# Scan decays of the prompt: running sums as head rows in two parts, one-hot and identity products, exponential straight from the bank

## The chip, the cores and the metric

The kernel runs as one program on 1 core of a Trainium2 chip. The metric is the device time of the program in microseconds (us). TensorE (PE in the profile; PEld for its weight loads), VectorE (DVE), ScalarE (ACT), GpSimd (POOL) and the DMA engines work side by side; each runs its own list of instructions in order and waits for others through semaphores.

## The reference, cut to what matters

One layer of a hybrid decoder, for a prompt of 256 tokens and 8 sample tokens. The change concerns the state-space branch of the prompt. It has 32 heads in 4 groups, a head width of 64, and chunks of 128 tokens:

```python
acum = cumsum(dt * a)                         # per head, within a chunk
seg = acum[t] - acum[s]
decay = exp(where(t >= s, seg, -inf))
wts = cb[t, s] * decay * dt[s]                # cb: product of C and B, per group
y_diag = wts @ x
decay_end = exp(acum[-1] - acum)
states = B^T (decay_end * dt * x);  h = h * exp(acum[-1]) + states
y = y_diag + (C h_prev) * exp(acum) + d * x
```

The kernel treats the 256 prompt tokens as one chunk, which gives the same values: a head then has a 256 x 256 lower triangle of decays, cut into three 128 x 128 blocks. With s on the partitions they are s in the first half against t in the first and in the second half, and s in the second half against t in the second. Beside this the layer has window attention, attention over a memory, gates, an output projection and a mixture of 32 experts (two for each token).

## The kernel before

All activations are kept transposed, with features on the partitions and 264 tokens (256 + 8) in a row. Weights come in chunks of 1 MB (256 columns) into three buffers W, loaded by SyncE in the order of use. The order of all work is written out by hand, engine by engine; `opened`, `full`, `drains`, `wait_filled` and `wait_drained` hand the eight matmul banks over between the engines.

**Split tiles.** The products with the memory weights and with the x/B/C, k, q and mq columns are computed in float32r, in two parts. For each 128 columns ScalarE makes the high part (`highs`, L1264), and GpSimd (`lows`) or, for some, VectorE (`vector_lows`) subtracts it from the weight to make the low part (`low_part`, L229). TensorE then makes 3 x 8 products (L469), and ScalarE copies the result out (`evac`, L1237). The normed inputs are split in the same way by VectorE (L1510, L1511); the first split tile waits for `mem_normed`, which the low part of the memory input gives. The columns of z and of the gates use plain float32 (L457).

**`rstd`** (L1239) is used 23 times: it loads a table set, then takes Ln of a sum of squares in a bank, then Exp. Each call has a table load at L1242.

**The scan stage** lies in the loop over the 40 tiles of z and the gates, TensorE's at L785, with its counterparts at L1344 (ScalarE) and L1758 (VectorE). Step i on TensorE: the tile zg i (eight products, L457); for i < 8 `ssd_bcast(i)`; for 1 <= i < 9 `ssd_y(i - 1)`; for i < 12 the two products `qk(i)` (L628, L630). A unit u is four heads. In it:

- `ssd_bcast` (L596) spreads dt*a of a head over all partitions as a weight and multiplies it with the triangle table: the running sum of the head, as a row, in every partition. Two heads share a bank, in banks 3 and 4.
- VectorE's `segments` (L1635) subtracts the running sum of the partition's own token (AC) and limits the result at 0, eight operations for a unit, into a tile D in S (two buffers).
- ScalarE takes the exponential of all of D (1536 columns) in one instruction (L1350), after copying out the tile zg i, and goes on to `rstd` of the q/k squares, for which it waits for VectorE's `qk_ready` of the step before.
- VectorE's `decays` (L1656), at the start of the next step, multiplies D with CB. CB is the product of C and B, already multiplied with the triangle at L1632.
- `ssd_y` (L609) multiplies D with XD, 64 columns of weights a head, and VectorE's `y_add` adds it to C. Then VectorE rotates q or k (`rotate`, L1669), which needs `rstd`.

At i = 10 to 13 TensorE makes the end states (L640), which wait for XD weighed by VectorE (L1771). At i = 12 and 13 the mq columns are normed: squares on TensorE (L478), four `rstd`, two VectorE products each (L1777). When the last state has been copied out, GpSimd stores them (L1195) and decays the first two sample states (L1207, 2048 columns each). From i = 14 on window attention, memory attention and the eight sample states follow in the same loop, then the branch projections, the output projection and the experts.

Of the kernel before, what the change touches and what calls it, by code (L numbers as in the profile page):

```python
# [8 lines left out]
P = 128  # L9
D_MODEL = 1024  # L10
SEQ = 256
# [119 lines left out]
def build_program(nc, ins, outs):  # L131
    ctx = ExitStack()
    with ctx:
# [22 lines left out]
        for off in (at_xd, at_xd + 1024, at_xd + 2048, at_xd + 3072, at_x + 5120, at_g):  # L156
            under_name(off, KT * P)
        M = ctx.enter_context(nc.sbuf_tensor("M", [P, top], F32))
# [77 lines left out]
        KSQ, QSQ = tiles("G", T, 2760, 3816), tiles("G", T, 3816, 5928)  # L236

# [189 lines left out]
        def _(pe):  # L427
# [111 lines left out]
            for i in range(4):  # L539
                for c in range(2):  # L540
                    split_tile(("q", 2 * i + c), c, HN_SPLIT, T, ("q", i))
                if i == 1:

                    pe.wait_ge(sem("dta"), 1)
                    b = opened("acum", 3)
                    pe.matmul(b[:, 0:32], tab("causal")[:, 0:P], DTA[:, 0, :], start=True, stop=True)
                    pe.matmul(b[:, 32:64], ones, DTA[:, 0, :], start=True, stop=False)
                    pe.matmul(b[:, 32:64], tab("causal")[:, 0:P], DTA[:, 1, :], start=False, stop=True)
                    pe.matmul(b[:, 64:96], ones, DTA[:, 0, :], start=True, stop=False)
                    full(pe.matmul(b[:, 64:96], ones, DTA[:, 1, :], start=False, stop=True), "acum")  # L550

                    pe.wait_ge(sem("dt_expanded"), 1)
                    b = opened("ex", 4)
                    for a, src in enumerate((DTX, DAX)):
                        for j in range(XS_T):
                            c0 = (a * XS_T + j) * BATCH_S
                            mm = pe.matmul(b[:, c0:c0 + BATCH_S], src[:, P * j:P * (j + 1)], ident[0:8, 0:8],
                                           start=True, stop=True)
                    full(mm, "ex")


            for i in range(4):
                for c in range(2):
# [23 lines left out]
                    if j == 5:  # L587

                        for g in range(4):
                            b = opened(("cb", g), 3 + g)  # L590
                            pe.matmul(b[:, 0:SEQ], C[:, XS_T + g, 0:P], C[:, XS_T + 4 + g, 0:SEQ],
                                      start=True, stop=True)
                            full(pe.matmul(b[:, SEQ:3 * P], C[:, XS_T + g, P:SEQ], C[:, XS_T + 4 + g, P:SEQ],
                                           start=True, stop=True), ("cb", g))

            def ssd_bcast(u):  # L596

                for a in range(2):
                    b = opened(("acb", u, a), 3 + a)
                    for q in range(2):  # L600
                        h = 4 * u + 2 * a + q
                        o = b[:, SEQ * q:SEQ * (q + 1)]
                        pe.matmul(o, DTA[:, 0, h:h + 1].to_broadcast([P, P]), tab("causal")[:, 0:SEQ],
                                  start=True, stop=False)
                        mm = pe.matmul(o[:, P:SEQ], DTA[:, 1, h:h + 1].to_broadcast([P, P]),
                                       tab("causal")[:, 0:P], start=False, stop=True)
                    full(mm, ("acb", u, a))

            def ssd_y(u):  # L609
# [3 lines left out]
                for q in range(4):  # L613
                    h = 4 * u + q
                    o = b[64 * (q % 2):64 * (q % 2) + 64, SEQ * (q // 2):SEQ * (q // 2 + 1)]
                    pe.matmul(o, XD[:, 0, HEADDIM * h:HEADDIM * (h + 1)], D[:, q, 0:SEQ], start=True, stop=False)
                    mm = pe.matmul(o[:, P:SEQ], XD[:, 1, HEADDIM * h:HEADDIM * (h + 1)], D[:, q, SEQ:3 * P],
                                   start=False, stop=True)
# [166 lines left out]
            for i in range(40):  # L785
# [446 lines left out]
        def _(act):  # L1232
# [5 lines left out]

            def rstd(name, dst, width, n):  # L1239
# [48 lines left out]
            def silu_conv(batch):  # L1288
                act.wait_ge(sem("convolved"), batch + 1)
                v = C[:, 8 * batch:8 * (batch + 1), :]  # L1290
                a.activation(v, v, ACT.Silu).then_inc(sem("conv_active"), 1)

# [40 lines left out]
            act.wait_ge(sem("to_end"), 1)  # L1333
            a.activation(WE, WE, ACT.Exp).then_inc(sem("end_decay"), 1)
            for j in range(8):
                evac(("mq", j), MQ[:, j, :], T)
                highs(52 + j + 3)
                if j == 4:
# [5 lines left out]
            for i in range(42):  # L1344
                if i < 40:
                    evac(("zg", i), Z[:, i, :] if i < 16 else G[:, i - 16, :], T)
                if i < 8:
                    act.wait_ge(sem("segments"), i + 1)
                    D = at("S", 1536 * (i % 2), 1536 * (i % 2 + 1))
                    a.activation(D, D, ACT.Exp).then_inc(sem("decay_exp"), 1)  # L1350
# [57 lines left out]
                if i == 28:  # L1408
                    wait_drained(act, ("zg", 15))
                    a.activation(at("Z"), at("Z"), ACT.Silu).then_inc(sem("z_active"), 1)  # L1410
                if i == 31:
# [79 lines left out]
        def _(dve):  # L1491
# [117 lines left out]
            link(v.tensor_copy(at("AC"), b[:, 0:64]))  # L1609
            drains(v.tensor_tensor(WE, each(b[:, 64:96], 2), AC, ALU.subtract), "acum")  # L1610
# [24 lines left out]
            def segments(u):  # L1635

                if u >= 2:
                    wait_filled(dve, ("y", u - 2))
                D = tiles("S", 3 * P, 1536 * (u % 2), 1536 * (u % 2 + 1))
                for a_ in range(2):  # L1640
                    b = wait_filled(dve, ("acb", u, a_))
                    for q in range(2):
                        h = 4 * u + 2 * a_ + q
                        o = b[:, SEQ * q:SEQ * (q + 1)]
                        v.tensor_scalar(D[:, 2 * a_ + q, 0:SEQ], o, AC[:, 0, h:h + 1], 0.0,
                                        ALU.subtract, ALU.min)
                        last = v.tensor_scalar(D[:, 2 * a_ + q, SEQ:3 * P], o[:, P:SEQ], AC[:, 1, h:h + 1], 0.0,
                                               ALU.subtract, ALU.min)
                    if a_ == 0:
                        drains(last, ("acb", u, 0))  # L1650

                drains(last, ("acb", u, 1))
                wait_drained(dve, ("acb", u, 1))
                done(dve, v.tensor_scalar(at("ST", 60, 61), AC[:, 0, 0:1], 0.0, None, ALU.mult), "segments")

            def decays(u):  # L1656
                dve.wait_ge(sem("decay_exp"), u + 1)
# [495 lines left out]
```

## Time and profile before

| | |
|---|---|
| median of 3 runs | 1034.17 us (1033.91 to 1037.94) |
| the profiled execution's own time | 1034.25 us |
| its span | 1032.4 us |
| TensorE busy, products / weight loads | 925.0 us (90%) / 723.4 us (70%) |
| VectorE busy | 460.8 us (45%) |
| ScalarE busy | 261.7 us (25%) |
| GpSimd busy | 189.3 us (18%) |
| data moved | 223.41 MB, 216 GB/s on average |
| table loads at L1242 | 23, mean 1283 ns |
| mean granted TensorE clock | 0.921 of full speed |

The span runs from the first to the last instruction that the profile shows; the time of the execution is 1.85 us longer. A busy share is the part of the span in which an engine has something in work. A product's duration in a timeline row includes its way through the array, so the pace of a row of products is read from the start of one row to the start of the next, not from durations. In a row, x16 is the number of merged records; an instruction at the border of two rows can be told in both. What stands in brackets is idle time of the engine before the row and what released it.

### The profile page before, as it was taken

How to read it: one execution, taken by the hardware profiler on the slowest of the kernel's cores; microseconds unless marked ns; L12 is line 12 of the kernel's file. 1: busy time of each engine (PE TensorE's matmuls, PEld its weight loads, DVE VectorE, ACT ScalarE, POOL GpSimd, SP SyncE). 2: the span in 40 equal slices, each digit the busy share in tenths (PEclk: the TensorE clock that was granted, in tenths of full speed). 3: DMA queues.
4: the chain of work that ended last, by engine and by line, in shares of the span. 5: the costliest groups of instructions: out<-in, count | busy, mean ns of one | idle time of the engine just before them, and what ended most of it. 6: DMA issues, size and time to landing. Idle time of an engine off the chain costs nothing. (4 is left out here: it accounts for less than half of the span.)

```text
span 1032.4 us, 14711 instructions
## 1 busy us (share of the span) xinstructions
PE 925.0 (90%) x6134; PEld 723.4 (70%) x6134; DVE 460.8 (45%) x800; ACT 261.7 (25%) x448; POOL 189.3 (18%) x91
## 2 busy tenths in 40 slices
PE   4899968899999896887879999999996999998888
PEld 3899968799988784554657677888785655554454
DVE  3621988932277636685376941111214122222222
ACT  5347433335344453322123230000001001010100
POOL 2347754326300003022212320000000000000000
PEclk9899988979999997898889999999995799998899
DMA  6354713323522213664556979547463479999992
GB/s 248 135 203 134 275 52 117 136 83 123 169 82 83 67 62 123 243 241 164 167 204 202 377 242 398 213 175 273 145 263 123 164 325 421 422 422 422 422 422 116
DMA packets 33640, 223.41 MB, mean 216 GB/s; under 512 B 3776, under 2 KB 4048, under 8 KB 9008
## 3 DMA queue, kind: packets, MB, share of 16 engines
q1 hardware_dynamic: 28048, 199.57, 49.8%
q0 software_dynamic: 5536, 23.06, 6.8%
q8 instruction: 40, 0.66, 0.2%
q14 instruction: 16, 0.13, 0.0%
HBM read 207.29 MB, written 15.31 MB: 216 GB/s over the span
## 5 line engine op out<-in xcount | busy, mean ns | idle before, releaser
L469 PE MATMUL bank<-at_r,at_r 128*128 128x264 f32 (+1 forms) x1152 | 153.9, 297 | 23.4 <-POOL at_r L229 16.2
L469 PEld LDWEIGHTS bank<-at_r,at_r 128*128 128x128 f32 x1152 | 150.3, 200 | 25.6 <-POOL at_r L229 18.0
L457 PE MATMUL bank<-HN,W 128*128 128x264 f32 x640 | 157.4, 401 | 0.0
L229 POOL TENSOR_TENSOR at_r<-W,at_r 128x1024 fp32r<-128x1024 f32 x52 | 128.3, 2473 | 124.3 <-ACT at_r L1264 124.2
L457 PEld LDWEIGHTS bank<-HN,W 128*128 128x128 f32 x640 | 124.5, 198 | 30.8 <-issue 9.6
L1237 ACT ACTIVATE M<-bank 128x264 f32<-128x264 f32 (+4 forms) x140 | 59.2, 429 | 256.1 <-PE bank L469 101.5
L457 PE MATMUL bank<-M,W 128*128 128x264 f32 x384 | 87.7, 388 | 4.0 <-DMA W<-in_w_stream 1.6
L926 PE MATMUL bank<-M,W 128*128 128x128 f32 (+1 forms) x432 | 83.1, 326 | 3.3 <-DVE M L1977 3.3
L457 PEld LDWEIGHTS bank<-M,W 128*128 128x128 f32 x384 | 72.2, 190 | 17.3 <-DMA W<-in_w_stream 2.5
L926 PEld LDWEIGHTS bank<-M,W 128*128 128x128 f32 (+1 forms) x432 | 63.5, 202 | 24.6 <-issue 6.7
L1264 ACT ACTIVATE at_r<-W 128x1024 fp32r<-128x1024 f32 x60 | 62.5, 1053 | 0.6 <-DMA W<-in_w_stream 0.5
L944 PE MATMUL bank<-M,W 128*32 128x256 f32 x1024 | 58.5, 387 | 0.9 <-DVE W L1987 0.9
L856 PE MATMUL bank<-M,W 128*128 128x264 f32 x256 | 57.1, 386 | 0.0
L856 PEld LDWEIGHTS bank<-M,W 128*128 128x128 f32 x256 | 48.6, 190 | 8.3
L944 PEld LDWEIGHTS bank<-M,W 128*32 128x32 f32 x1024 | 32.6, 112 | 25.7 <-issue 5.4
L1552 DVE SCALAR_TENSOR_TENSOR M<-M 128x255 f32<-128x255 f32 (+2 forms) x72 | 50.4, 771 | 0.3
L1242 ACT ACT_TABLE_LOAD x23 | 29.5, 1283 | 76.1 <-PE bank L478 61.5
L967 PE MATMUL bank<-M,W 128*32 128x512 f32 x256 | 36.8, 728 | 13.1 <-DMA M<-in_w_exp_down 11.2
L713 PE MATMUL bank<-M 8*128 8x512 f32 x32 | 24.5, 906 | 20.2 <-DVE M L1692 12.1
L1207 POOL TENSOR_TENSOR M<-M 128x2048 f32<-128x2048 f32 x8 | 34.9, 4374 | 39.4 <-DMA M<-in_state_ssm 39.4
L1987 DVE COPY W<-bank 128x512 f32<-128x512 f32 x9 | 6.2, 692 | 78.4 <-PE bank L926 78.4
L979 PE MATMUL bank<-M,W 128*128 128x264 f32 x128 | 37.1, 412 | 1.8
(318 smaller groups left out, 1086.1 us busy)
## 6 DMA issues: line engine op xcount, KB each, us to landing
W<-in_w_stream SPq DMA_DIRECT2D x70, 1024.0 KB, 4.9
M<-in_w_exp_gate SPq DMA_DIRECT2D x32, 1024.0 KB, 22.7
M<-in_w_exp_up SPq DMA_DIRECT2D x32, 1024.0 KB, 23.7
M<-in_w_exp_down SPq DMA_DIRECT2D x32, 1024.0 KB, 15.7
M<-in_state_ssm POOLq DMA_DIRECT2D x8, 1024.0 KB, 7.6
M<-in_mem_kT SPq DMA_DIRECT2D x8, 1024.0 KB, 5.9
out_s_ssm<-M POOLq DMA_DIRECT2D x8, 1024.0 KB, 11.7
M<-in_mem_v SPq DMA_DIRECT2D x8, 1024.0 KB, 7.2
```

What stands on the lines that cost most here:

```text
L229: return eng.tensor_tensor(low, x, high.bitcast(F32), ALU.subtract)
L457: mm = pe.matmul(bank[:, 0:n], w[:, k, P * c:P * (c + 1)], x[:, k, 0:n], start=(k == 0), stop=(k == KT - 1))
L469: mm = pe.matmul(bank[:, 0:n], w[:, k, :], x_[:, k, 0:n], start=(k + i == 0), stop=(k == KT - 1 and i == 2))
L856: mm = pe.matmul(banks[c][:, 0:T], w[:, k, P * c:P * (c + 1)], C[:, KT * part + k, :], start=(part + k == 0), stop=(part == 1 and k == KT ...
L926: mm = pe.matmul(psum[4 + k // 4][:, P * (k % 4):P * (k % 4 + 1)], HTOK[0:rows, t, P * k:P * (k + 1)], ONE[0:rows, t].rearrange("p j s -> ...
L944: mm = pe.matmul(psum[bank][SLOTS * j:SLOTS * (j + 1), 0:D_FF], HG[:, k, SLOTS * j:SLOTS * (j + 1)], piece(kind, buf, j)[:, k, :], start=( ...
L967: mm = pe.matmul(psum[2 + half][SLOTS * j:SLOTS * (j + 1), :], ACTT[:, f, SLOTS * j:SLOTS * (j + 1)], piece("down", buf, j)[:, f, 512 * ha ...
L979: pe.matmul(psum[6 + m % 2][:, 0:T], DOWNED[:, P * m:P * (m + 1)], BACK, start=True, stop=True).then_inc(sem("tile_filled"), 1)
L1207: nc.gpsimd.tensor_tensor(H, H, EX[:, 1, :, b].unsqueeze(2).to_broadcast([P, XS_T, STATE]), ALU.mult).then_inc(sem("state_decayed"), 1)
L1237: drains(a.activation(dst, b[0:rows, 0:n] if src is None else src(b), ACT.Copy), name)
L1264: a.activation(like_raw(w_split(name, c)[0], name), raw_half(name, c), ACT.Copy).then_inc(sem(f"high_ready{c}"), 1)
L1552: last = v.scalar_tensor_tensor(C[:, j, back:SEQ], X[:, j, 0:SEQ - back], tap(j, 3 - back), C[:, j, back:SEQ], ALU.mult, ALU.add)
```

## The change

1. Running sums as rows (TensorE): four float32 products behind `acum` in the q stage put the running sums of the 32 heads as rows into bank 7, once on partitions 0 to 31 and once on 32 to 63.
2. Two parts and tables: between mq tiles 6 and 7 ScalarE copies these rows in float32r (the high part, ACUM, three blocks of 128 columns), and makes in float32r the tables NOT_YET (0 where t >= s, else -1e30), IDENT_R (the identity) and HEAD (the identity twice, one column a head). VectorE replaces partitions 32 to 63 of ACUM with the low part. They lie where weight parts of the mq tiles lay.
3. `ssd_bcast` makes, for each head, one float32r product of HEAD's column (spread over 128) with ACUM, 64 rows deep and 384 columns wide, and adds one of IDENT_R with NOT_YET, 256 columns wide. A head has a bank of its own: heads 0 and 2 of a unit use bank 3, heads 1 and 3 bank 4. Heads 0 and 1 now come ahead of the tile zg i, heads 2 and 3 behind it.
4. ScalarE takes the exponential straight from the bank, two instructions a head (256 and 128 columns), with the negated AC as bias, and hands the bank back. VectorE's `segments` goes, with its small operation at L1654. The limit at 0 goes with it; CB is copied and no longer multiplied by the triangle; D's blocks lie in another order, with strided operands.
5. `rstd` loads its table set only when another set may have come between: 2 of the 23 loads stay. The load before the exponential of WE is written out.

The core of the diff:

```diff
@@ TensorE, q stage, behind acum
+                    b = opened("acum_rows", 7)
+                    for r0 in (0, 32):
+                        rows = b[r0:r0 + 32, :]
+                        pe.matmul(rows[:, 0:SEQ], DTA[:, 0, :], tab("causal")[:, 0:SEQ], start=True, stop=False)
+                        mm = pe.matmul(rows[:, P:SEQ], DTA[:, 1, :], tab("causal")[:, 0:P], start=False, stop=True)
+                    full(mm, "acum_rows")
@@ TensorE, loop
-            def ssd_bcast(u):
-
-                for a in range(2):
-                    b = opened(("acb", u, a), 3 + a)
-                    for q in range(2):
-                        h = 4 * u + 2 * a + q
-                        o = b[:, SEQ * q:SEQ * (q + 1)]
-                        pe.matmul(o, DTA[:, 0, h:h + 1].to_broadcast([P, P]), tab("causal")[:, 0:SEQ],
-                                  start=True, stop=False)
-                        mm = pe.matmul(o[:, P:SEQ], DTA[:, 1, h:h + 1].to_broadcast([P, P]),
-                                       tab("causal")[:, 0:P], start=False, stop=True)
-                    full(mm, ("acb", u, a))
+            def ssd_bcast(u, heads):
+
+                if u == 0 and heads[0] == 0:
+                    wait_drained(pe, "acum_rows")
+                    pe.wait_ge(sem("decay_tables"), 1)
+                for q in heads:
+                    h = 4 * u + q
+                    b = opened(("acb", h), 3 + q % 2)
+                    pe.matmul(b[:, 0:3 * P], HEAD[:, h:h + 1].to_broadcast([64, P]), ACUM, start=True, stop=False)
+                    full(pe.matmul(b[:, 0:2 * P], IDENT_R, NOT_YET, start=False, stop=True), ("acb", h))
...
+                if i < 8:
+                    ssd_bcast(i, (0, 1))
                 feature_tile(("zg", i), w, i % 2, HN, T, name)
                 if i < 8:
-                    ssd_bcast(i)
+                    ssd_bcast(i, (2, 3))
@@ ScalarE, rstd
-                a.preload_act_table_set("natural_log_exp_and_others")
+                if not logs_loaded[0]:
+                    a.preload_act_table_set("natural_log_exp_and_others")
+                    logs_loaded[0] = True
@@ ScalarE, mq stage
+                if j == 6:
+
+                    b = wait_filled(act, "acum_rows")
+                    a.activation(ACUM[:, 0:SEQ], b[0:64, 0:SEQ], ACT.Copy)
+                    a.activation(ACUM[:, SEQ:3 * P], b[0:64, P:SEQ], ACT.Copy).then_inc(sem("acum_high"), 1)
...
+                    a.activation(IDENT_R, ident, ACT.Copy)
...
@@ ScalarE, loop
-                    act.wait_ge(sem("segments"), i + 1)
-                    D = at("S", 1536 * (i % 2), 1536 * (i % 2 + 1))
-                    a.activation(D, D, ACT.Exp).then_inc(sem("decay_exp"), 1)
+                    if i >= 2:
+                        wait_filled(act, ("y", i - 2))
+                    D = tiles("S", 3 * P, 1536 * (i % 2), 1536 * (i % 2 + 1))
+                    for q in range(4):
+                        h = 4 * i + q
+                        b = wait_filled(act, ("acb", h))
+                        first, seg = (x.rearrange("p (k w) -> p k w", w=P)[:, 0::2, :] for x in (D[:, q, :], b[:, 0:3 * P]))
+                        a.activation(first, seg, ACT.Exp, bias=AC[:, 0, h:h + 1])
+                        last = a.activation(D[:, q, P:2 * P], b[:, P:2 * P], ACT.Exp, bias=AC[:, 1, h:h + 1])
+                        drains(last, ("acb", h))
@@ VectorE
-                drains(v.tensor_tensor(CB[:, g, :], b[:, 0:3 * P], tab("causal"), ALU.mult), ("cb", g))
+                drains(v.tensor_copy(CB[:, g, :], b[:, 0:3 * P]), ("cb", g))
...
+            dve.wait_ge(sem("acum_high"), 1)
+            low = decay_r[32:64, 0:3 * P]
+            b = psum[7]
+            for to, of in ((slice(0, SEQ), slice(0, SEQ)), (slice(SEQ, 3 * P), slice(P, SEQ))):
+                last = low_part(v, low[:, to], b[32:64, of], low[:, to])
+            drains(last, "acum_rows")
...
-                if i < 8:
-                    segments(i)
```

## Rows read from the trace of the kernel before

**Rows 1.** The page, part 4: the chain that ended last, by line.
```profile
DMA M<-in_w_exp_down 9%; PE bank L457 7%; PE bank L856 6%; PE bank L926 5%; PE bank L967 4%; PE bank L944 3%; DMA out_s_ssm<-M 2%; DMA M<-in_state_ssm 2%; DMA W<-in_w_stream 1%; DMA out_s_swa_v<-M 1%; PE bank L979 1%; POOL M L1207 1%; PE bank L478 1%; SPq L1069 1%; DVE HN L2011 1%
```

**Rows 2.** Timeline of TensorE, one step: start us, us, engine, line, operation, tiles, count.
```profile
290.35 3.72 PE L457 MATMUL bank<-HN,W 128*128 128x264 f32 x16
293.91 0.59 PE L603 MATMUL bank<-M 128*128 128x256 f32 x2
296.78 0.66 PE L616 MATMUL bank<-M 128*64 128x256 f32 x4
298.28 0.71 PE L628 MATMUL bank<-M 128*128 128x264 f32 x2
299.27 1.94 PE L457 MATMUL bank<-HN,W 128*128 128x264 f32 x8
```

**Rows 3.** Timeline of ScalarE, same step; idle before and its releaser in brackets.
```profile
299.68 1.48 ACT L1350 ACTIVATE M<-M 128x1536 f32<-128x1536 f32 x1 [4.86 <-DVE M L1654]
```

**Rows 4.** Timeline of VectorE, same step.
```profile
294.97 1.76 DVE L1659 TENSOR_TENSOR M<-M 128x1536 f32<-128x1536 f32 x1
303.42 0.43 DVE L1677 TENSOR_TENSOR M<-M 128x264 f32<-128x264 f32 x1 [1.59 <-ACT M L1245]
```

**Rows 5.** Timeline of TensorE, float32r tiles of the mq stage.
```profile
250.09 3.19 PE L469 MATMUL bank<-at_r,at_r 128*128 128x264 f32 x24
253.12 1.03 PE L572 MATMUL bank<-M 128*128 128x128 f32 x8
```

**Rows 6.** Timeline of ScalarE: a copy with its successor, and exponentials that accumulate.
```profile
231.57 0.39 ACT L1237 ACTIVATE M<-bank 128x264 f32<-128x264 f32 x1 [14.76 <-PE bank L469]
231.86 1.05 ACT L1264 ACTIVATE at_r<-W 128x1024 fp32r<-128x1024 f32 x1
...
402.16 0.40 ACT L1386 ACTIVATE M<-M 128x128 f32<-128x128 f32 x1 [2.53 <-DVE M L1699]
415.74 0.51 ACT L1386 ACTIVATE M<-M 128x256 f32<-128x256 f32 x1 [4.77 <-DVE M L1699]
416.15 0.19 ACT L1386 ACTIVATION_READ_ACCUMULATOR M<-M 128x1 f32 x1
```

**Rows 7.** Timeline of TensorE, the last unit, and one row of the windows view.
```profile
343.88 3.72 PE L457 MATMUL bank<-HN,W 128*128 128x264 f32 x16
350.31 0.84 PE L616 MATMUL bank<-M 128*64 128x256 f32 x4 [2.70 <-DVE M L1659]
354.41 3.72 PE L457 MATMUL bank<-HN,W 128*128 128x264 f32 x16
...
350.00:355.00 5.00, 4.69 (x23) 3.52 (x24) 1.51 (x4) 0.85 (x1) 0.00 (x0) 0.66 0.00 0
```

**Rows 8.** Timeline of all engines, 386 to 402 us: mq scaling, state decay.
```profile
387.59 1.28 ACT L1242 ACT_TABLE_LOAD   x1 [0.34 <-PE bank L478]
389.05 7.24 POOL L1207 TENSOR_TENSOR M<-M 128x2048 f32<-128x2048 f32 x2
389.83 7.17 DVE L1777 SCALAR_TENSOR_TENSOR M<-M 128x264 f32<-128x264 f32 x2 [3.02 <-ACT M L1245]
401.12 1.21 PE L713 MATMUL bank<-M 8*128 8x512 f32 x1 [8.51 <-DVE M L1692]
```

**Rows 9.** Timeline of all engines, first stage.
```profile
17.92 1.28 ACT L1242 ACT_TABLE_LOAD   x1 [1.24 <-PE bank L478]
21.40 2.29 DVE L229 TENSOR_TENSOR at_r<-HN,at_r 128x2048 fp32r<-128x2048 f32 x1
22.18 3.75 POOL L229 TENSOR_TENSOR at_r<-W,at_r 128x1024 fp32r<-128x1024 f32 x1 [5.20 <-ACT at_r L1264]
23.75 8.68 PE L469 MATMUL bank<-at_r 128*128 128x256 f32 x48 [5.91 <-DVE at_r L229]
```

**Rows 10.** Windows: busy us (count) per engine, granted clock, DMA share, GB/s.
```profile
90.00:92.00 2.00, 2.00 (x19) 2.00 (x18) 0.00 (x0) 1.88 (x3) 1.27 (x1) 1.00 0.02 8
92.00:94.00 2.00, 1.92 (x16) 1.71 (x15) 0.00 (x0) 0.86 (x2) 2.00 (x2) 1.00 0.00 0
```

More of the change, by code:

```diff
@@ L236, in build_program @@
         KSQ, QSQ = tiles("G", T, 2760, 3816), tiles("G", T, 3816, 5928)
+        ACUM = decay_r[0:64, 0:3 * P]
+        NOT_YET = decay_r[:, 3 * P:5 * P]
+        IDENT_R = decay_r[:, 5 * P:6 * P]
+        HEAD = decay_r[0:64, 6 * P:6 * P + SSM_HEADS]
         DTX, DAX = at("XD", 0, 2048, 8), at("XD", 2048, 4096, 8)
@@ L590, in _ @@
                             b = opened(("cb", g), 3 + g)
[L591 to L593 removed]
+                            first = b[:, 0:3 * P].rearrange("p (k w) -> p k w", w=P)[:, 0::2, :]
+                            pe.matmul(first, C[:, XS_T + g, 0:P], C[:, XS_T + 4 + g, 0:SEQ], start=True, stop=True)
+                            full(pe.matmul(b[:, P:2 * P], C[:, XS_T + g, P:SEQ], C[:, XS_T + 4 + g, P:SEQ],
                                            start=True, stop=True), ("cb", g))
[L596 to L607 removed]
+            def ssd_bcast(u, heads):
[7 more added lines that the diff above has]
+                    full(pe.matmul(b[:, 0:2 * P], IDENT_R, NOT_YET, start=False, stop=True), ("acb", h))
             def ssd_y(u):
@@ L615, in ssd_y @@
                     o = b[64 * (q % 2):64 * (q % 2) + 64, SEQ * (q // 2):SEQ * (q // 2 + 1)]
-                    pe.matmul(o, XD[:, 0, HEADDIM * h:HEADDIM * (h + 1)], D[:, q, 0:SEQ], start=True, stop=False)
-                    mm = pe.matmul(o[:, P:SEQ], XD[:, 1, HEADDIM * h:HEADDIM * (h + 1)], D[:, q, SEQ:3 * P],
+                    first = D[:, q, :].rearrange("p (k w) -> p k w", w=P)[:, 0::2, :]
+                    pe.matmul(o, XD[:, 0, HEADDIM * h:HEADDIM * (h + 1)], first, start=True, stop=False)
+                    mm = pe.matmul(o[:, P:SEQ], XD[:, 1, HEADDIM * h:HEADDIM * (h + 1)], D[:, q, P:2 * P],
                                    start=False, stop=True)
@@ L1291, in silu_conv @@
                 a.activation(v, v, ACT.Silu).then_inc(sem("conv_active"), 1)
+                logs_loaded[0] = False
             for j in range(CONV_T):
@@ L1333, in _ @@
             act.wait_ge(sem("to_end"), 1)
+            a.preload_act_table_set("natural_log_exp_and_others")
+            logs_loaded[0] = True
             a.activation(WE, WE, ACT.Exp).then_inc(sem("end_decay"), 1)
@@ L1337, in _ @@
                 highs(52 + j + 3)
+                if j == 6:
+                    b = wait_filled(act, "acum_rows")
+                    a.activation(ACUM[:, 0:SEQ], b[0:64, 0:SEQ], ACT.Copy)
+                    a.activation(ACUM[:, SEQ:3 * P], b[0:64, P:SEQ], ACT.Copy).then_inc(sem("acum_high"), 1)
+                    a.activation(NOT_YET.rearrange("p (k w) -> p k w", w=P),
+                                 tab("causal").rearrange("p (k w) -> p k w", w=P)[:, 0::2, :], ACT.Copy,
+                                 scale=1e30, bias=-1e30)
+                    a.activation(IDENT_R, ident, ACT.Copy)
+                    for r0 in (0, 32):
+                        last = a.activation(HEAD[r0:r0 + 32, :], ident[r0:r0 + 32, r0:r0 + 32], ACT.Copy)
+                    last.then_inc(sem("decay_tables"), 1)
                 if j == 4:
@@ L1608, in _ @@
             b = wait_filled(dve, "acum")
-            link(v.tensor_copy(at("AC"), b[:, 0:64]))
-            drains(v.tensor_tensor(WE, each(b[:, 64:96], 2), AC, ALU.subtract), "acum")
+            link(v.tensor_scalar(at("AC"), b[:, 0:64], -1.0, None, ALU.mult))
+            drains(v.tensor_tensor(WE, each(b[:, 64:96], 2), AC, ALU.add), "acum")
             wait_drained(dve, "acum")
@@ L1631, in _ @@
                 b = wait_filled(dve, ("cb", g))
-                drains(v.tensor_tensor(CB[:, g, :], b[:, 0:3 * P], tab("causal"), ALU.mult), ("cb", g))
+                drains(v.tensor_copy(CB[:, g, :], b[:, 0:3 * P]), ("cb", g))
                 wait_drained(dve, ("cb", g))
[L1635 to L1654, printed above, removed]
+            dve.wait_ge(sem("acum_high"), 1)
[4 more added lines that the diff above has]
+            drains(last, "acum_rows")
+            wait_drained(dve, "acum_rows")
             def decays(u):
-                dve.wait_ge(sem("decay_exp"), u + 1)
+                wait_drained(dve, ("acb", 4 * u + 2))
+                wait_drained(dve, ("acb", 4 * u + 3))
                 D = tiles("S", 3 * P, 1536 * (u % 2), 1536 * (u % 2 + 1))
```

3 lines of the change are left out of this document (added).

## The prediction, made before the changed kernel was built or run

> **What bounds the kernel now.** I read the page of busy shares first: TensorE is busy for 90% of the span, so anything that gives it time can count. The chain that ended last comes second: it is a mixture, matmuls and the landings of expert weights, with state stores and loads between [rows 1]. The chain does not go through the scan stage by name, so I read that stage itself, in the timelines. One step of the z loop (one output tile and four heads) is, on TensorE [rows 2]: the tile from 290.35 to 293.91 (3.56 us), the eight plain float32 broadcast products from 293.91 to the y products at 296.78 (2.87 us, of which by the even pace of 0.655 a head 2.62 is work and 0.25 waiting), y 1.50, the two q/k products 0.99: a period of 8.92 us. VectorE and ScalarE go round in the same 8.92 us [rows 3, 4]: the decay multiply at 294.97, four heads of segments, the big exponential at 299.68 (1.48), a table load (1.28), Ln, Exp, the last rotate at 303.42, and the next multiply. So two chains of nearly equal length meet here. A change on one side alone would give little; this one shortens both.
>
> **The change, part by part.**
>
> *The broadcasts.* A float32 pass over 384 columns costs 0.655 us. The new products are float32r. That kind runs 24 products of 264 columns from 250.09 to 253.12: 0.126 us each [rows 5]. 264 columns at 2.4 GHz are 0.110, so about 0.016 is on top. The new head is one product of 384 columns (0.160 + 0.016) and one of 256 (0.107 + 0.016): 0.30 us. Four heads are 1.20 us in place of 2.62.
>
> *The bank handoff, a new wait.* Heads 2 and 3 use the banks of heads 0 and 1, which only ScalarE now empties, and ScalarE does that after copying out the tile that TensorE made between them. Behind the waiting product stand y of the step before and the q/k products, and VectorE waits for those. From the end of the tile: about 0.07 to start the copy, 0.29 until the next instruction [rows 6]. An exponential of 256 columns lets the next in after about 0.27 and one of 128 after 0.17, by the slope of the copy and the big exponential (1.48 for 1536); from above, with the accumulating exponentials of the attention, 0.41 (415.74 to 416.15) and, as much before its end, 0.31 [rows 6]. Head 0's bank is free some 0.9 to 1.0 after the tile's end, head 1's at 1.35, and head 3's products end at 1.7. Of those 1.7 us 0.6 is work and 1.1 is TensorE idle. I take the lower costs, since the new instructions accumulate nothing; by the upper, 1.7 becomes 2.3.
>
> *The new period* is 0.6 (heads 0, 1) + 3.56 + 1.7 + 1.50 + 0.99 = 8.35 us. Is something else late? From the q/k products VectorE needs three multiplies of some 0.45 and, with ScalarE's Ln and Exp done meanwhile without a table load, the last rotate, some 1.9, then the multiply 1.76: 3.65 us, and y is reached 5.9 after them. VectorE loses its segments and has 2 us to spare. ScalarE does about 3.1 us of 8.35. TensorE alone sets the period. From the mq tile's end at about 273.78 (the first tile starts at once) the new order gives q/k of unit 0 at 280.5, unit 1 at 288.9, unit 7 six periods later at 339.0. Before, it was 343.88 [rows 7]: 4.9 us gained.
>
> *The last unit.* Before, TensorE ended tile 8 at 347.44 and stood until 350.31; the granted clock of the stretch after is 0.66 on average, so part of y and q/k ran at 1.2 GHz, and tile 9 began at 354.41 [rows 7]: 10.53 us. Now the multiply is ready 3.65 after the q/k products and the tile takes 3.56: 3.56 + 0.2 + 1.50 + 0.99 = 6.25. Gained 4.3; together 9.2. If the clock fell all the same, 1.6 less.
>
> *Table loads.* 21 of the 23 loads before an Ln go. Twelve lie in the loop and are counted above. Of the mq ones, one ends at 388.87 and delays VectorE's products to 389.83, behind GpSimd's state decay, which started at 389.05; VectorE then finishes only at about 397.0, a second load follows, and TensorE waits until 401.12 [rows 8]. The second load gives 1.28. The first lets VectorE start at 388.55: its second product would start at about 389.0, just ahead of GpSimd or just behind. Ahead, all is 3.1 us earlier; behind, 1.3. Too close to call: 2.2.
>
> *The early load costs.* Without the load at 17.92 ScalarE's highs come 1.28 earlier, and GpSimd, which started its low at 22.18 and took 3.75 because VectorE's low (21.40, 2.29) was running, comes at 20.9, ahead of VectorE [rows 9]. A free one of that kind takes 2.3 or so (3.75 less the 1.5 it stood). VectorE's low would wait until 23.2 at least and end at 25.5 instead of 23.69, and TensorE's first split tile stands behind exactly that, at 23.75. That is +1.8 us; if the cast before it also keeps GpSimd out until 21.37, +2.25. I take +2.0, bounds 0 (the highs wait for a chunk) and 2.3. This delay moves the whole kernel, since the tiles, copies and highs that follow hang on one another.
>
> The Trainium skill, SBUF — State Buffer, "SBUF: two separate sides", says that VectorE in a two-port mode or with two SBUF inputs and GpSimd take an exclusive lock for a whole instruction. By that rule the cast holds it too, and the term is 2.25 in place of 1.8.
>
> *Loads at the memory keys.* Four go, 5.1 us of ScalarE earlier. Between 92 and 94 TensorE has 16 products, against 19 in the window before: 3 x 0.126 = 0.35 us lost to late lows [rows 10]. Gained 0.35, bounds 0 and 0.4.
>
> *Running sums.* Four float32 products of 32 columns wide weights go into the q stage, on TensorE's path: two pairs. Pairs that use different column groups, as y, cost 0.375 each [rows 2], pairs that don't 0.655: 0.75 to 1.31. I take +0.8.
>
> *At nothing:* six copies on ScalarE and two subtractions on VectorE between mq tiles 6 and 7, some 1.4 and 0.8 us long beside a tile of 3 us; uncovered, they would delay the first broadcast by 1 us. Negated AC, copied CB, strided blocks: as long as before, within 0.2 us.
>
> Sum: -9.2 - 2.2 + 2.0 - 0.35 + 0.8 = -8.95. The profiled execution took 1034.25 (span 1032.4), 0.08 off the median shown, 1034.17; so the sum gives 1025.2.
>
> **Does it arrive at the end?** From 400 on each wait hangs on an earlier release: state stores on VectorE's add, the expert loads on TensorE's uses. No engine and no queue follows a clock of its own, so the shift should pass, within 3 us either way for collisions of transfers.
>
> **The rivals.**
> *A, as forecast:* 1025.
> *B, ScalarE's small exponentials cost as the accumulating ones* [rows 6]: the period is 8.95, the 4.9 us go, 1030. For it: two instructions per head reading a bank with a bias from memory; against it: the copies' 0.29.
> *C, the new idle time drops the clock (slower).* Each step now has 1.1 us of idle just ahead of the y products. Rows show a fall after 2.9 us of idle [rows 7], none in this stage while it was almost gapless [rows 2]. A tile of 3.56 us would take twice that at 1.2 GHz; a dip over half a tile in each of eight steps costs 8 x 1.8 = 14 us: 1039. It decides from 1.1 us a step on (8.95 / 8).
> The Trainium skill, TensorE: Matmul & The Clock Gate, "A second HAM failure mode: psum-queue depth-cycling", says that short waits between groups of products, from cycling through banks, can make the clock oscillate. In stages before with shorter gaps the trace doesn't show it; with this gap it is untried.
> *D, the shift is swallowed behind 400:* store and load of states take turns with weights [rows 1], and a worse interleaving gives the 9 us back: 1034.
> *E, more:* GpSimd does not get ahead early and VectorE does later: -2.0 and -0.9: 1022.
>
> **Chances.** A 0.52, B 0.13, C 0.09, D 0.11, E 0.15. The likeliest gives 1025. With 1 us more than E and short of D, the range is 1018 to 1032; what it leaves out is C, D and a little of the rest. A measurement here can tell 0.5% (5.2 us) from nothing: faster means under 1029. Faster 0.76 (A nearly whole, E, a third of B, none of C or D), same 0.15, slower 0.09.
>
> **What would show it.** Float32r broadcasts of 0.30 us a head; an idle of about 1.1 us ahead of head 2 of each unit, released by ScalarE; tiles 8.35 us apart, against 8.92; y of unit 7 with hardly a wait and the clock at full; TensorE's first split tile near 25.7; VectorE's mq products ending 1.3 or 3.1 earlier. It would be wrong if tiles stood 8.9 apart (B), if the granted clock fell below 1.0 in the loop (C), or if everything up to 400 is 9 us earlier and the end is not (D).

## The result, and the profile after

The changed kernel is slower: 1050.89 us in the median of its runs (1050.13 to 1051.16) against 1036.06 (1033.91 to 1040.1) for the kernel before, measured again beside it; the ratio is 1.0132 with a 95% interval of 1.0097 to 1.0167. The forecast was 1025.2 with a range of 1018 to 1032. It is missed, and on the other side.

The page of the changed kernel, its first lines:

```profile
span 1049.0 us, 14570 instructions
## 1 busy us (share of the span) xinstructions
PE 929.8 (89%) x6078; PEld 716.7 (68%) x6078; DVE 441.9 (42%) x730; ACT 245.6 (23%) x489; POOL 188.2 (18%) x91
```

VectorE (460.8 before) and ScalarE (261.7) have less to do, as meant. TensorE should have lost about 11 us of broadcast work and has 4.8 more (925.0 before). Now the step of the z loop, TensorE, start and duration as in [rows 2]:

```profile
299.55 0.44 PE L617 MATMUL bank<-at_r 64*128 64x384 f32 x1
299.92 0.38 PE L618 MATMUL bank<-at_r 128*128 128x256 f32 x1
300.23 0.44 PE L617 MATMUL bank<-at_r 64*128 64x384 f32 x1
300.60 0.39 PE L618 MATMUL bank<-at_r 128*128 128x256 f32 x1
300.83 3.72 PE L464 MATMUL bank<-HN,W 128*128 128x264 f32 x16
305.72 0.44 PE L617 MATMUL bank<-at_r 64*128 64x384 f32 x1 [1.16 <-ACT M L1389]
...
307.08 0.66 PE L628 MATMUL bank<-M 128*64 128x256 f32 x4
308.59 0.71 PE L640 MATMUL bank<-M 128*128 128x264 f32 x2
309.67 0.44 PE L617 MATMUL bank<-at_r 64*128 64x384 f32 x1
```

L617 is the head product and L618 the one with the identity; L464 is the tile, L628 y and L640 the q/k products. From head 0 of this step to head 0 of the next it is 309.67 - 299.55 = 10.12 us; forecast were 8.35, and before it was 8.92. A head takes 0.37 + 0.31 = 0.68 us, not 0.30: as much as the float32 products it replaced (0.655). The weight loads of the same stretch show why the duration of the product itself is not to blame:

```profile
299.92 0.19 PEld L618 LDWEIGHTS bank<-at_r 128*128 128x128 f32 x1 [0.19 <-issue]
300.23 0.18 PEld L617 LDWEIGHTS bank<-at_r 64*128 64x128 f32 x1
300.60 0.19 PEld L618 LDWEIGHTS bank<-at_r 128*128 128x128 f32 x1 [0.19 <-issue]
```

Each load starts only when its own product is due (299.92 in both views), and not beside the product before it. ScalarE between the tile and head 2:

```profile
304.65 0.39 ACT L1251 ACTIVATE M<-bank 128x264 f32<-128x264 f32 x1 [4.53 <-PE bank L464]
304.94 0.47 ACT L1388 ACTIVATE M<-bank,M 128x256 f32<-128x256 f32 x1
305.29 0.37 ACT L1389 ACTIVATE M<-bank,M 128x128 f32<-128x128 f32 x1
305.54 0.48 ACT L1388 ACTIVATE M<-bank,M 128x256 f32<-128x256 f32 x1
```

Twice the granted clock also fell to its lower level in the loop. The windows view (the third number from the end of a row is the granted clock), and the tile that lay in the first fall:

```profile
284.00:286.00 2.00, 1.96 (x8) 1.34 (x8) 0.00 (x0) 1.78 (x6) 0.00 (x0) 1.00 0.60 170
286.00:288.00 2.00, 2.00 (x5) 0.86 (x3) 1.29 (x3) 0.95 (x3) 0.00 (x0) 0.52 0.01 4
...
338.00:340.00 2.00, 2.00 (x16) 1.54 (x12) 0.00 (x0) 0.36 (x2) 0.00 (x0) 0.50 1.02 430
```

```profile
288.58 5.86 PE L464 MATMUL bank<-HN,W 128*128 128x264 f32 x16
```

By the granted clock of such windows the first fall lasts from about 286.1 to 292.9 and the second from about 337.3 to 340.7. TensorE was at work, without a bracket, for the 2 us before the first one; its last idle time had been that ahead of head 2, at 284.04. By the length of their steps beside the plain ones the falls cost 3.0 and 1.6 us, 4.5 together before rounding.

The last unit, which was 10.53 us [rows 7], is 368.08 - 361.69 = 6.39:

```profile
361.69 3.72 PE L464 MATMUL bank<-HN,W 128*128 128x264 f32 x16
365.58 0.66 PE L628 MATMUL bank<-M 128*64 128x256 f32 x4 [0.17 <-DVE M L1687]
...
368.08 0.39 PE L464 MATMUL bank<-HN,W 128*128 128x264 f32 x1
```

The first stage, where [rows 9] had TensorE at 23.75, one row each of GpSimd, VectorE and TensorE:

```profile
21.00 2.51 POOL L230 TENSOR_TENSOR at_r<-W,at_r 128x1024 fp32r<-128x1024 f32 x1 [4.09 <-ACT at_r L1282]
```
```profile
21.35 4.31 DVE L230 TENSOR_TENSOR at_r<-HN,at_r 128x2048 fp32r<-128x2048 f32 x1
```
```profile
25.71 1.65 PE L476 MATMUL bank<-at_r 128*128 128x256 f32 x6 [7.78 <-DVE at_r L230]
```

And the mq products, where [rows 8] had 389.83 and 7.17 on VectorE and TensorE at 401.12 after 8.51 of idle. GpSimd's decays, VectorE, TensorE:

```profile
402.35 7.24 POOL L1221 TENSOR_TENSOR M<-M 128x2048 f32<-128x2048 f32 x2
```
```profile
401.85 8.44 DVE L1803 SCALAR_TENSOR_TENSOR M<-M 128x264 f32<-128x264 f32 x2 [4.30 <-ACT M L1263]
```
```profile
413.13 1.22 PE L725 MATMUL bank<-M 8*128 8x512 f32 x1 [7.22 <-DVE M L1720]
```

Where the time went, by TensorE's landmarks, after minus before:

| landmark | before | after | difference |
|---|---|---|---|
| first split tile | 23.75 | 25.71 | +2.0 |
| first `acum` product | 215.28 | 218.42 | +3.1 |
| behind the running sums | 216.41 | 220.33 | +3.9 |
| first work of unit 0 (tile before, head 0 after) | 273.78 | 277.81 | +4.0 |
| tile 8 | 343.88 | 361.69 | +17.8 |
| tile 9 | 354.41 | 368.08 | +13.7 |
| first sample product | 401.12 | 413.13 | +12.0 |
| eighth sample product | 592.03 | 605.15 | +13.1 |
| first branch projection | 679.5 | 694.7 | +15.2 |
| first expert product | 792.2 | 807.1 | +14.9 |
| span | 1032.4 | 1049.0 | +16.6 |

Between unit 0 and tile 8, 13.8 us are lost where 4.9 were to be won, and what stands at tile 9 reaches the end; where the 4.6 us that are added behind the first sample product come from was not found.

These are one execution of each kernel, and ahead of the loop that matters. The kernels of the experiments called k128, pairs and order differ from the changed kernel there by two small copies or not at all, and yet unit 0 begins at 276.49, 278.08 and 273.57 in them, against 277.81. In order the granted clock is 1.00 from 50 to 60 us, where the changed kernel's profile has 0.55 and 0.76. So the +4.0 ahead of the loop is not a price that the change always pays; the loop's 13.8 us are more than this spread.

### The profile page after: what moved, and what is told of

Its sections match the earlier page's. It is cut to its first block and busy times, and to the rows that moved or that the text cites. A ratio compares the mean times of both kernels' runs of the same rounds, so it can differ in the third digit from the quotient of the medians.

```text
span 1049.0 us, 14570 instructions
## 1 busy us (share of the span) xinstructions
PE 929.8 (89%) x6078; PEld 716.7 (68%) x6078; DVE 441.9 (42%) x730; ACT 245.6 (23%) x489; POOL 188.2 (18%) x91
## 5 line engine op out<-in xcount | busy, mean ns | idle before, releaser
L464 PE MATMUL bank<-HN,W 128*128 128x264 f32 x640 | 161.8, 410 | 0.0
L464 PEld LDWEIGHTS bank<-HN,W 128*128 128x128 f32 x640 | 127.1, 203 | 31.9 <-issue 9.8
L464 PE MATMUL bank<-M,W 128*128 128x264 f32 x384 | 87.7, 388 | 4.9 <-DMA W<-in_w_stream 2.6
L464 PEld LDWEIGHTS bank<-M,W 128*128 128x128 f32 x384 | 72.2, 190 | 18.2 <-DMA W<-in_w_stream 3.4
L870 PEld LDWEIGHTS bank<-M,W 128*128 128x128 f32 x256 | 48.6, 190 | 8.3
L981 PE MATMUL bank<-M,W 128*32 128x512 f32 x256 | 36.9, 727 | 13.8 <-DMA M<-in_w_exp_down 12.0
L725 PE MATMUL bank<-M 8*128 8x512 f32 x32 | 22.1, 825 | 18.4 <-DVE M L1720 10.9
L993 PEld LDWEIGHTS bank<-M,W 128*128 128x128 f32 x128 | 19.7, 188 | 22.9 <-DVE HN L2037 11.8
```

The source lines that it names most:

```text
L464: mm = pe.matmul(bank[:, 0:n], w[:, k, P * c:P * (c + 1)], x[:, k, 0:n], start=(k == 0), stop=(k == KT - 1))
L870: mm = pe.matmul(banks[c][:, 0:T], w[:, k, P * c:P * (c + 1)], C[:, KT * part + k, :], start=(part + k == 0), stop=(part == 1 and k == KT ...
L981: mm = pe.matmul(psum[2 + half][SLOTS * j:SLOTS * (j + 1), :], ACTT[:, f, SLOTS * j:SLOTS * (j + 1)], piece("down", buf, j)[:, f, 512 * ha ...
L993: pe.matmul(psum[6 + m % 2][:, 0:T], DOWNED[:, P * m:P * (m + 1)], BACK, start=True, stop=True).then_inc(sem("tile_filled"), 1)
```

## The experiments

All are compared with the kernel before on the same chip: a ratio is the time over that of the kernel before, and the two numbers behind it are its 95% interval. Its median there was 1038.06 for the first four and 1038.66 for the last four. Where an expectation speaks of a theory D, it is the one of row depth (a change between products 64 and 128 rows deep leaves the weight load uncovered), not the prediction's rival D.

### Head products as deep as the rest (k128)

```diff
+        ACUM_DEEP = decay_r[:, 0:3 * P]
+        HEAD_DEEP = decay_r[:, 6 * P:6 * P + SSM_HEADS]
-                    pe.matmul(b[:, 0:3 * P], HEAD[:, h:h + 1].to_broadcast([64, P]), ACUM, start=True, stop=False)
+                    pe.matmul(b[:, 0:3 * P], HEAD_DEEP[:, h:h + 1].to_broadcast([P, P]), ACUM_DEEP, start=True, stop=False)
+                    a.activation(ACUM_DEEP[64:128, :], tab("causal")[64:128, :], ACT.Copy, scale=0.0)
+                    a.activation(HEAD_DEEP[64:128, :], ident[64:128, 0:SSM_HEADS], ACT.Copy)
```

The 64 rows more are zeros, so the sums stay the same.

> The changed kernel with the head products 128 rows deep in place of 64: rows 64 to 127 of the one-hot table and of the running-sum rows are zero, so the result is the same. In the changed kernel a head costs 0.68 us, 0.37 + 0.31, and a weight load of 0.19 us stands uncovered ahead of nearly every product. Theory D (depth): the load is uncovered because products of 64 and of 128 rows take turns. Then a head costs 0.30, heads 0 and 1 of a unit 0.6 in place of 1.28, tiles come 9.05 us apart in place of 10.12, and the kernel takes about 1042 us. Theory S (short runs or spread weights): float32r products wait for their weights here whatever their depth; then a head stays at 0.68, the distance at 10.1 and the time at 1051.

Measured: 1037.25 us (1029.66 to 1041.05), ratio 0.9974, 0.9941 to 1.0006. TensorE's rows:

```profile
301.16 0.71 PE L642 MATMUL bank<-M 128*128 128x264 f32 x2
...
302.45 0.33 PE L619 MATMUL bank<-at_r 128*128 128x384 f32 x1
302.62 0.28 PE L620 MATMUL bank<-at_r 128*128 128x256 f32 x1
302.74 3.72 PE L466 MATMUL bank<-HN,W 128*128 128x264 f32 x16
307.62 0.45 PE L619 MATMUL bank<-at_r 128*128 128x384 f32 x1 [1.16 <-ACT M L1393]
```
```profile
302.45 0.19 PEld L620 LDWEIGHTS bank<-at_r 128*128 128x128 f32 x1
```

From 302.45 to 302.74 one head takes 0.29 us, what the prediction had, and the load of L620 starts 0.17 ahead of its product at 302.62, beside the one before. Nothing but the depth differs in the loop, so the 0.39 by which a head is longer in the changed kernel are the two changes of depth in it, 0.19 to 0.20 each. The whole stretch says the same: from the q/k products to the tile it is 302.74 - 301.16 = 1.58 us here and 310.95 - 308.59 = 2.36 in the changed kernel, 0.78 less for four changes fewer. The step is 9.07, as expected, and not the 8.35 of the prediction: the idle time of 1.16 ahead of head 2 stays, and head 3 now waits as well. All ten-us windows from 284 to 344 are at clock 1.00 here; the two falls that are missing (4.5 us) are about the 5 us by which the time is below the expected 1042. So an idle time of 1.16 in every step does not by itself bring the clock down.

### Both head products, then both identity products (pairs)

```diff
+                banks = []
                 for q in heads:
...
+                    banks.append(opened(("acb", h), 3 + q % 2))
+                    pe.matmul(banks[-1][:, 0:3 * P], HEAD[:, h:h + 1].to_broadcast([64, P]), ACUM, start=True, stop=False)
+                for q, b in zip(heads, banks):
+                    h = 4 * u + q
+                    full(pe.matmul(b[:, 0:2 * P], IDENT_R, NOT_YET, start=False, stop=True), ("acb", h))
```

> The changed kernel with the order of products inside a pair of heads changed: both head products (64 rows), then both identity products (128 rows), so the depth changes half as often. Theory D: of four uncovered loads in a pair two go, 1.28 us becomes about 0.95 ahead of the tile; behind the tile the second head product waits for its bank, so nothing is gained there; tiles 9.8 us apart, 1048 us. Theory S: all loads stay uncovered, 10.1 us apart, 1051 us.

Measured: 1045.89 us (1043.09 to 1047.46), ratio 1.0057, 1.0023 to 1.0092; the step is 9.78. TensorE:

```profile
303.65 0.43 PE L618 MATMUL bank<-at_r 64*128 64x384 f32 x1 [1.16 <-ACT M L1392]
...
307.66 0.61 PE L618 MATMUL bank<-at_r 64*128 64x384 f32 x2
308.21 0.51 PE L621 MATMUL bank<-at_r 128*128 128x256 f32 x2
308.55 2.84 PE L464 MATMUL bank<-HN,W 128*128 128x264 f32 x12
```

Heads 0 and 1 take 308.55 - 307.66 = 0.89 in place of 1.28: two changes of depth fewer, 0.39 less. That is the same price from the other side, with the products untouched. For heads 2 and 3 the gain is lost to the wait for head 1's bank.

### The handoff away from the path (order)

```diff
-                if i < 8:
-                    ssd_bcast(i, (0, 1))
                 feature_tile(("zg", i), w, i % 2, HN, T, name)
                 if i < 8:
-                    ssd_bcast(i, (2, 3))
+                    ssd_bcast(i, (0, 1))
...
                     qk(i)
+                if i < 8:
+                    ssd_bcast(i, (2, 3))
```

ScalarE takes the exponentials of heads 2 and 3 after `rstd` of the step.

> The changed kernel with the products left as they are and only moved, so that no bank is asked for while ScalarE still has the tile's copy and exponentials to do: tile, heads 0 and 1, y of the unit before, q/k products, heads 2 and 3. ScalarE takes the exponentials of heads 2 and 3 after rstd. Theory H (handoff): TensorE's idle time of 1.2 us a step goes and tiles come 3.56 + 1.28 + 1.50 + 1.08 + 1.36 = 8.8 us apart; with the idle time gone the two falls of the clock in the loop (3.0 and 1.6 us) go too: about 1037 us. Rival: the exponentials of heads 2 and 3 come too late behind rstd and the decay multiply for the next y, and the distance stays near 10 us, 1049 us.

Measured: 1036.16 us (1029.83 to 1040.41), ratio 0.9964, 0.9927 to 1.0002. TensorE:

```profile
302.14 0.44 PE L617 MATMUL bank<-at_r 64*128 64x384 f32 x1
...
307.36 3.72 PE L464 MATMUL bank<-HN,W 128*128 128x264 f32 x16
311.01 0.43 PE L617 MATMUL bank<-at_r 64*128 64x384 f32 x1
```

No bracket is left on TensorE's products in the step, which is 311.01 - 302.14 = 8.87 us. The handoff was worth 10.12 - 8.87 = 1.25 a step, and the clock no longer falls in these eight steps.

### Part 5 alone on the kernel before (loads_only)

```diff
-                a.preload_act_table_set("natural_log_exp_and_others")
+                if not logs_loaded[0]:
+                    a.preload_act_table_set("natural_log_exp_and_others")
+                    logs_loaded[0] = True
```

With it the written-out load ahead of the exponential of WE, as in the change.

> The kernel before with part 5 of the change alone (21 of the 23 table loads go). Theory L (lock): the early one costs 2 us at TensorE's first split tile, since GpSimd's low part comes ahead of VectorE's. In the loop the circle through VectorE and ScalarE is 1.3 us shorter, so TensorE sets 8.7 us a step: 1.7 us gained, 1.3 to 2.9 at the last unit, 1.3 at the mq products. Sum about -3: 1033 us against 1036 for the kernel before. Rival: without the early loss 1031.

Measured: 1033.37 us (1032.22 to 1039.64), ratio 0.9953, 0.9924 to 0.9983. The step is 8.77 against 8.92; the first split tile comes at 25.82, 2.07 late; the sample product stands 2.8 ahead. The last unit, from tile 8 to tile 9 on TensorE:

```profile
345.22 3.72 PE L457 MATMUL bank<-HN,W 128*128 128x264 f32 x16
349.14 0.66 PE L616 MATMUL bank<-M 128*64 128x256 f32 x4 [0.20 <-DVE M L1667]
...
351.64 1.05 PE L457 MATMUL bank<-HN,W 128*128 128x264 f32 x4
```

It takes 6.42 us, where 1.3 to 2.9 less than 10.53 were expected: as short as the changed kernel's 6.39, with `segments` still in place. So the whole gain of the change at the last unit is that of the table loads. They were the part of the change that paid, by about 0.5% of the time.

### Order and depth together (order_k128)

The edits of order and k128 in one kernel.

> The moved order of run order together with the 128 rows deep head products of run k128. Both theories (depth, handoff) hold apart from each other: then a step is 3.56 + 0.6 + 1.50 + 1.08 + 0.6 = 7.35 us against 8.87 in run order and 9.07 in run k128, and the kernel takes about 1025 us, beside 1037 for those two. Rival: the circle through rstd, the exponentials of heads 2 and 3 and the decay multiply is the next limit and holds the step at 8.0 or more, 1030 us.

Measured: 1023.95 us (1019.12 to 1026.86), ratio 0.9874, 0.9824 to 0.9924. TensorE:

```profile
301.31 3.72 PE L466 MATMUL bank<-HN,W 128*128 128x264 f32 x16
...
308.62 1.72 PE L466 MATMUL bank<-HN,W 128*128 128x264 f32 x7
```

The step is 308.62 - 301.31 = 7.31 us. Alone, depth gave 1.05 and order 1.25; together they give 2.81, since in k128 the shorter heads were partly eaten by the wait for a bank. On top of order, depth gives 8.87 - 7.31 = 1.56 us: eight changes in a step fewer, 0.195 each, which is the price of a change for the third time.

### The early table load kept (xload), and all three (best)

```diff
+            logs_loaded[0] = False
             rstd("ss_x", RS, D_MODEL, T)
```

> The changed kernel with that one table load kept and nothing else altered. Theory L: first split tile near 23.75 us, GpSimd's low at 22.2 with some 3.75 us, and the time 1 to 2 us below the changed kernel's 1051: 1049. Rival (the delay had another cause): the tile stays at 25.7, 1051 us.

Measured: 1048.2 us (1043.98 to 1049.79), ratio 1.0083, 1.0052 to 1.0115. GpSimd, VectorE, TensorE:

```profile
22.82 3.48 POOL L230 TENSOR_TENSOR at_r<-W,at_r 128x1024 fp32r<-128x1024 f32 x1 [5.78 <-ACT at_r L1282]
```
```profile
21.79 2.29 DVE L230 TENSOR_TENSOR at_r<-HN,at_r 128x2048 fp32r<-128x2048 f32 x1
```
```profile
24.13 2.08 PE L476 MATMUL bank<-at_r 128*128 128x256 f32 x8 [5.66 <-DVE at_r L230]
```

With the load back, GpSimd's low starts after VectorE's, VectorE's takes 2.29 again instead of 4.31, and the tile comes 1.58 earlier. The early cost was the order in which two engines arrive, and a table load had set it. All the kernels here without that load start the tile at 25.7 to 26.4, and the three with it at 23.75 to 24.13. In the whole time the two intervals (this one and the changed kernel's) overlap: it is shown in the trace, not in the total.

> As run order_k128, with the table load at the input's sum of squares kept, so that GpSimd's first contended low part comes behind VectorE's. Theory L (lock): TensorE's first split tile starts near 23.75 in place of 25.7, and 1 to 2 us of it last to the end: 1023 us. Rival: the gain is used up by the low clock after it and nothing is left: 1025 us.

Measured (order, k128 and xload in one): 1020.3 us (1019.27 to 1022.98), ratio 0.9828, 0.979 to 0.9865. This beats both kernels; from order_k128 it can't be told apart. The traces say why: the first split tile is 1.9 us earlier than in order_k128 (23.82 against 25.72), but tile 0 of the loop comes 2.9 us later (276.25 against 273.38), with the clock at 0.50 from 50 to 55 us against 1.00. The rival named ahead of the run, a gain used up by the low clock, is what these two profiles show.

Of the 16.5 us that it stands ahead at the first sample product (384.62 against 401.12) 11.2 arrive at the end. 4.8 of them go at one place, where the last values of the ring come from a small transfer: 3.8 in longer idle time and 1.1 in slower products. TensorE of best, then of the kernel before:

```profile
591.28 3.02 PE L786 MATMUL bank<-M 128*32 128x128 f32 x64 [4.21 <-DMA M<-M]
```
```profile
602.75 1.95 PE L772 MATMUL bank<-M 128*32 128x128 f32 x64 [0.44 <-DMA M<-M]
```

The idle time is 7.12 in order and 1.67 in the changed kernel. It does not come from TensorE being early alone: xload, where TensorE is as late as in the changed kernel (617.36), has 4.20. Behind the idle time the same 64 products take 3.02 instead of 1.95; in order, where they take 3.64, the granted clock of the ten us around them is 0.79. Why the transfer comes when it does was not looked into.

### The bias left out (nobias)

```diff
-                        a.activation(first, seg, ACT.Exp, bias=AC[:, 0, h:h + 1])
-                        last = a.activation(D[:, q, P:2 * P], b[:, P:2 * P], ACT.Exp, bias=AC[:, 1, h:h + 1])
+                        a.activation(first, seg, ACT.Exp)
+                        last = a.activation(D[:, q, P:2 * P], b[:, P:2 * P], ACT.Exp)
```

The decays are then not those of the reference: the running sum of the partition's own token is not subtracted.

> The changed kernel with the bias left out of the small exponentials, so the decays are not those of the reference (the partition's own running sum is not subtracted); it only measures what the bias costs. A pair of exponentials (256 and 128 columns) goes by in 0.60 us in the changed kernel, where I had reckoned 0.44. Theory bias: reading one value per partition from memory is the rest, and the pair falls to 0.44. Rival: the strided read of the bank or the smaller size costs it, and it stays at 0.60. Tiles stay 9.9 to 10.1 us apart by either, about 1050 us.

Measured, in one run: 1047.87 us. ScalarE:

```profile
301.27 0.38 ACT L1388 ACTIVATE M<-bank 128x256 f32<-128x256 f32 x1
301.54 0.28 ACT L1389 ACTIVATE M<-bank 128x128 f32<-128x128 f32 x1
301.69 0.40 ACT L1388 ACTIVATE M<-bank 128x256 f32<-128x256 f32 x1
```

The pair takes 301.69 - 301.27 = 0.42 us (0.27 + 0.15) instead of 0.60 (0.35 + 0.25). The prediction's 0.27 + 0.17 is nearly right for exponentials without a bias from memory; the bias costs 0.08 to 0.10 an instruction.

## Why the prediction was wrong

**The step that failed is "The broadcasts": 0.30 us a head.** It measured 0.68. The sum had no term for a weight load that waits. The pace came from [rows 5], 24 products of one shape; the new ones change between 64 and 128 rows with every product. Three runs settle it: 0.39 less a head with equal depth (k128), 0.39 less a pair with two changes fewer (pairs), 1.56 less a step with eight fewer (order_k128 against order).

The trace of before had the row that warns, in the view of weight loads that I did not read: the first load after the y products, which use half the columns of the array, where the kind changes from 128*64 to 128*128.

```profile
297.70 0.41 PEld L617 LDWEIGHTS bank<-M 128*64 128x64 f32 x4
298.28 0.30 PEld L628 LDWEIGHTS bank<-M 128*128 128x128 f32 x2 [0.17 <-issue]
```

The Trainium skill, TensorEngine Tiling (Array Packing), "Key Properties", says it too: changing the tiling mode, and not just the tile, drains TensorE. The traces agree, with 0.17 to 0.19 us of uncovered load for a change.

**The handoff was named rightly and mis-sized.** From the end of the tile's pace (304.39) to head 2 at 305.72 it was 1.33 us, not the 0.9 to 1.0 of the prediction (0.97 is taken here). ScalarE begins its copy 0.26 after that point instead of 0.07; 0.16 of this is the last product's way through the array (the row ends at 304.55), which the sum left out. The exponential pair takes 0.60 instead of 0.44 (nobias). Together that is some 0.36 a step. The wait stood where the prediction put it, ahead of head 2 and released by ScalarE; head 3 had none, since a head takes longer than thought. Of the step's 1.77 us too many, 0.68 are heads 0 and 1, 0.36 the handoff, 0.63 heads 2 and 3 beyond what was planned for them, and 0.10 the q/k products, behind which the first change of depth lies. In eight steps the heads make 10.5 us, the handoff 2.9, the q/k products 0.8 and the clock 4.5: the 18.7 by which the loop missed (13.8 lost instead of 4.9 won).

**Rival C (the clock falls) was partly true:** in two of the eight steps, 4.5 us instead of 14. The kernels order, order_k128 and best, without the idle time, are at 1.00 in every ten-us window of these steps. Of those that have it, pairs falls twice (0.86 and 0.83 in the lowest windows), xload (0.68) and nobias (0.86) once each, and k128 stays at 1.00. The idle time goes with the falls and does not make one by itself; what decides was not found. **Rival B** (dearer exponentials) was true too, by the bias and not by accumulating, and smaller than the price it gave. **Rivals D and E** did not occur: from tile 9 to the end the shift goes from 13.7 to 16.6, 12.0 to 13.2 through the state stage. In the faster kernels a transfer near 600 takes back 4 to 7 us, as D had it of other transfers, but xload and pairs, which are not faster, stand 4.2 us there too.

**Right were:** the last unit (6.39, forecast 6.25, before 10.53), all of it by the table load, as loads_only shows; the early load at the first split tile (+1.96, forecast +2.0, by the mechanism forecast: GpSimd at 21.00 ahead of VectorE, whose low ends at 25.66); the running sums (+0.8, 219.55 to 220.33); the mq products in the case called "behind" (-1.3: VectorE started 0.5 ahead of GpSimd at 401.85, and its second product was still held until the decays ended, 8.44 in all; the sum had taken 2.2, between its two cases). The term of the memory keys was not measured by itself: from the first x/B/C tile to the dt products the difference falls from +2.18 to +1.16, where 0.35 was forecast.

That the early 2 us move the whole kernel did not hold so plainly: in order the first split tile is just as late (25.79), and the first x/B/C tile is 0.7 us ahead of the kernel before (80.40 against 81.10). Not foreseen were 2.0 us between the dt products (+1.16) and `acum` (+3.14): the last split tile waited 1.93 for GpSimd's low part and took 4.72 us at a granted clock of 0.60 and 0.55, against 0.41 and 3.18 before. These 2.0 us come and go too: k128, order and order_k128 do not have them.

The Trainium skill, SBUF — State Buffer, "SBUF: two separate sides", with its exclusive lock between VectorE and GpSimd, would have given 2.25 for the early load and the plain sum 1.8; the trace has 1.96 and so lies between the two. GpSimd's row starts at 21.00, inside the cast (20.09 to 21.32), and takes 2.51 us where the one before, without company, took 2.34: whether the cast held it stays open.

The sum again, with the terms of these two profiles: +2.0 and +1.9 in the early stages, +0.1 between the running sums and the loop, +13.8 in the eight steps, -4.1 for the last unit, -1.7 until the first sample product, +4.6 from there: +16.6 us, the difference of the spans.

## What to carry to other kernels

A product's price is that of its place in the row: before a pace is taken from rows of one shape, look whether the new ones change the tile of the array, and at the weight-load view for a gap ahead of the first load of a new shape. Here padding a short contraction with zero rows cost nothing in the loop and spared two changes a head; with an order that keeps ScalarE's handoff off TensorE's path it turned +1.3% into -1.3% (-1.7% with the early load kept, which can't be told apart). An instruction that only costs time, as a table load, can still hold another engine back to good effect: ask what comes first when it is gone. And a difference of a few us ahead of the changed stage has to be seen in more than one profile before it is called a cost of the change.

## What the hardware showed that was not expected

- A change of the tile between 64*128, 128*128 and 128*64 leaves 0.17 to 0.19 us of weight load uncovered at the full clock, and 0.195 us from start to start (after, k128, pairs, order_k128 against order, and the kernel before).
- A bias from memory costs an exponential out of a bank 0.08 to 0.10 us: 0.35 and 0.25 from start to start for 256 and 128 columns with it, 0.27 and 0.15 without.
- With 1.16 us of idle time in every step the granted clock fell twice in the eight steps in two kernels (after, pairs), once in two others (xload, nobias) and not at all in a fifth (k128).
- The same instructions ahead of the loop took up to 4.5 us more or less (unit 0 at 273.57 in order and at 278.08 in pairs), with the granted clock from 50 to 60 us at 1.00 in the one and at 0.61 and 0.71 in the other.
